# Attention in units of two heads, scores computed two units ahead, and the routing's Exp moved ahead of its token copies

## The reference

```python
probs = jax.nn.softmax(jnp.einsum('bnd,de->ben', h, router).astype(jnp.float32), axis=1)
gates, idx = lax.top_k(probs, cap)      # 16 experts, cap = 64 of 512 tokens
xs = h[bidx, idx]
```

## Time and profile before

| what | value |
|---|---|
| time, median of 3 runs | 2752.82 us (2751.13 to 2754.84) |
| the profiled execution's own time | 2752.04 us |
| its span | 2750.4 us |
| PE busy | 2445.9 us (89%) |
| DVE busy | 948.3 us (34%) |
| ACT busy | 497.1 us (18%) |
| HBM traffic | 202 GB/s over the span |

### The profile page before, as it was taken

One profiled execution on the slowest core, in us unless ns is written; L12 is line 12 of the kernel. 1 busy time (PEld: TensorE's weight loads), 2 busy tenths in 40 slices (PEclk: granted clock), 3 DMA queues, 4 the chain that ended last, 5 costly groups with the idle time before them and its releaser, 6 DMA issues.

```text
span 2750.4 us, 28001 instructions
## 1 busy us (share of the span) xinstructions
PE 2445.9 (89%) x11738; PEld 1060.6 (39%) x11738; DVE 948.3 (34%) x1631; ACT 497.1 (18%) x821; POOL 0.2 (0%) x4
## 2 busy tenths in 40 slices
PE   6899999599999988875999999889988699996698
PEld 1343345233333323332333333234433348644443
DVE  4547462411111125634011111131125745246551
ACT  2256100211110111022111111010023331124300
POOL 0000000000000000000000000000000000000000
PEclk9899999799999999977999999999998899996799
DMA  7236621599999972214899999812221120120062
GB/s 269 91 137 233 244 97 65 196 410 409 409 409 409 409 285 67 69 39 192 349 409 409 409 409 409 354 52 76 77 73 59 46 70 26 48 86 20 1 199 77
DMA packets 146010, 556.58 MB, mean 202 GB/s; under 512 B 13561, under 2 KB 14073, under 8 KB 138523
## 3 DMA queue, kind: packets, MB, share of 16 engines
q1 hardware_dynamic: 139584, 538.83, 51.2%
q10 hardware_dynamic: 6300, 15.95, 1.5%
HBM read 544.26 MB, written 10.49 MB: 202 GB/s over the span
## 4 chain that ended last, share of the span: by engine, by line
PE 74%; DVE 14%; DMA 6%; ACT 4%; issue 2%; ACTq 0%; DVEq 0%; SPq 0%
PE bank L204 72%; DMA experts<-in_exp_w 5%; PE bank L207 2%; DVE residual L1354 1%; DVE softmax L2407 1%; DVE rms L1670 1%; DMA residual<-in_w_mod 1%; DVE proj L423 0%; DVE scores L2413 0%; DVE topk L1248 0%; DVE max L1247 0%; DVE squares L1320 0%; ACT wring L1282 0%; ACT squares L1314 0%; ACT L1629 0%
## 5 line engine op out<-in xcount | busy, mean ns | idle before, releaser
L204 PE MATMUL bank<-normed,wring 128*128 128x512 f32 x1712 | 780.4, 608 | 23.7 <-DVE residual L1542 10.3
L204 PEld LDWEIGHTS bank<-normed,wring 128*128 128x128 f32 x1712 | 323.3, 193 | 425.7 <-issue 393.5
L204 PE MATMUL bank<-experts,wring 128*64 128x512 f32 x2048 | 449.6, 594 | 10.2 <-DMA experts<-in_exp_w 8.4
L204 PEld LDWEIGHTS bank<-experts,wring 128*64 128x64 f32 x2048 | 143.6, 137 | 301.2 <-issue 273.2
L1320 DVE TENSOR_TENSOR squares<-squares,bank 128x512 f32<-128x512 f32 x32 | 22.0, 688 | 688.6 <-ACT squares L1314 688.6
L204 PE MATMUL bank<-experts,hs_t 128*64 128x512 f32 x1024 | 224.1, 594 | 6.5 <-DMA experts<-in_exp_w 5.1
L204 PE MATMUL bank<-give_t,y 128*128 128x512 f32 x256 | 128.6, 621 | 10.3 <-DVE residual L1354 5.9
L204 PEld LDWEIGHTS bank<-experts,hs_t 128*64 128x64 f32 x1024 | 72.4, 137 | 147.0 <-issue 145.0
L1354 DVE SCALAR_TENSOR_TENSOR residual<-bank,mods,residual 128x512 f32<-128x512 f32 x128 | 96.1, 751 | 75.6 <-PE bank L204 69.8
L204 PE MATMUL bank<-h_tm,pick 128*128 128x512 f32 x256 | 116.8, 610 | 2.2 <-DVE pick L1262 2.2
L204 PE MATMUL bank<-proj,wring 128*128 128x512 f32 x224 | 99.4, 597 | 1.6 <-DVE proj L2470 1.6
(11 more groups left out here) (466 smaller groups left out, 2154.2 us busy)
## 6 DMA issues: line engine op xcount, KB each, us to landing
experts<-in_exp_w SPq DMA_DIRECT2D x384, 1024.0 KB, 18.4
wring<-in_w_in SPq DMA_DIRECT2D x82, 512.0 KB, 3.4
residual<-in_w_mod SPq DMA_DIRECT2D x40, 1024.0 KB, 7.0
wring<-in_cf_w SPq DMA_DIRECT2D x24, 512.0 KB, 3.4
wmod<-in_w_mod SPq DMA_DIRECT2D x8, 1024.0 KB, 10.2
merge_gates<-squares ACTq DMA_DIRECT2D x32, 256.0 KB, 3.1
merge_g<-merge_gates SPq DMA_DIRECT2D x8, 1024.0 KB, 6.5
wring<-in_w_out SPq DMA_DIRECT2D x14, 512.0 KB, 3.5
```

The lines of the kernel that those rows point to most:

```text
L204: return self.nc.tensor.matmul(out, lhsT, rhs, start=start, stop=stop, skip_group_check=True)
```

## The change

Two places are changed, and three constants with them.

Attention: 8 units (chunk c, head pair hp) replace the 16 heads. Banks 0 to 3 hold the scores of one unit, banks 4 to 7 the transposed weights and outputs. The matmuls of the two heads are issued alternately: for scores they lie on the upper and lower 64 rows of the array, for the weighted sum on the two halves of its columns. Maxima, reciprocals and gate products take both heads in one instruction. PE issues the scores of unit n+2 before the transposes of unit n; DVE issues bias and maxima of unit n+1, then the output of unit n-1, then the weights of unit n; ACT issues the Exp of unit n+1 before the copies of unit n. The three mask operations go: `cdist` now holds 1e30 where a compressed block isn't visible, and rows that see none get a gate of zero (`cseen`).

Routing: ACT runs a one-column Exp behind the shifts, then the softmax's Exp, then the eight copies. PE turns two of the eight token groups, then the probabilities, then the other six groups. DVE sets the ones while the Exp is awaited, reads the first round of the top-k straight from PSUM, and leaves out the subtraction of one, since `iota` now starts at 1.

```diff
@@ routing, tensor
+    tokens_tensor(k, m, 0)
     t.wait_ge(*k.at(f"{name}.softmax"))
     for n in range(NT):
         ins = k.turn(bank[2][0:NE, n * P:(n + 1) * P], m.pb[:, n, :])
     ins.then_inc(*k.up("tensor", f"{name}.probs"))
+    for n in range(1, NT):
+        tokens_tensor(k, m, n)
     t.wait_ge(*k.at(f"{name}.ranks"))
...
@@ routing, scalar
     modulate_scalar(k, f"{name}.h", lambda c: k.MOD[:, m.layer, 24 + c, 0:1], lambda c: k.H[:, c, :])
+    k.act(s.activation(k.SM[:, 62:63], k.con("ones", 0, 1), ACT.Exp))
+    s.wait_ge(*k.at(f"{name}.centred"))
+    k.act(s.activation(m.pb[:, :, :], m.pb[:, :, :], ACT.Exp), f"{name}.exp")
     for n in range(NT):
         for h in range(2):
             s.wait_ge(*k.at(f"{name}.h_tm{n}.{h}"))
             k.act(s.copy(m.ht[:, n, 512 * h:512 * h + 512], bank[4 + (2 * n + h) % 4][:, :]), f"{name}.ht{n}.{h}")
-    s.wait_ge(*k.at(f"{name}.centred"))
-    k.act(s.activation(m.pb[:, :, :], m.pb[:, :, :], ACT.Exp), f"{name}.exp")
@@ routing, vector
+    k.vec(v.memset(m.pet[:, :], 1.0))
     v.wait_ge(*k.at(f"{name}.exp"))
...
-    k.vec(v.tensor_copy(wk[:, 0, :], bank[2][0:NE, :]))
     for r in range(CAP // 8):
-        k.vec(v.max(m.mx[:, :], wk[:, r % 2, :]))
-        k.vec(v.match_replace(wk[:, (r + 1) % 2, :], m.mx[:, :], wk[:, r % 2, :], -1.0))
+        left = wk[:, r % 2, :] if r else bank[2][0:NE, :]
+        k.vec(v.max(m.mx[:, :], left))
+        k.vec(v.match_replace(wk[:, (r + 1) % 2, :], m.mx[:, :], left, -1.0))
...
-    k.vec(v.memset(m.pet[:, :], 1.0))
...
-    k.vec(v.tensor_scalar(wk[:, 0, :], wk[:, 0, :], -1.0, None, ALU.add), f"{name}.ranks")
```

More of the change, by code:

```diff
@@ L1580, in __init__ @@
         self.hc = n.sb("cmp_h", [P, 32])
[L1581 to L1584, removed]
+        self.sc = n.sb("scores", [P, 6, 512 + 384 + 32])
+        self.pt = n.sb("scores_t", [P, 2, 8 * P])
+        self.ms = n.sb("softmax", [P, 6, 6])
         mg = at.then()
@@ L2365, in head_scalar @@
[L2365 to L2380, removed]
-        k.act(s.copy(m.pt[:, u, i * P:(i + w) * P], bb[i // 4][:, 0:w * P]))
-    k.act(s.copy(m.pt[0:NCMP, u, j * P:(j + 1) * P], bb[j // 4][0:NCMP, (j % 4) * P:(j % 4 + 1) * P]), f"{name}.pt")
-    yield
-    yield
@@ new lines, in weights_vector @@
+def weights_vector(k, m, n):
+    v = k.nc.vector
+    c, hp, u = UNITS[n]
+    tot = m.ms[:, u:u + 2, 3:6]
+    v.wait_ge(*k.at(f"at{n}.exp"))
+    k.vec(v.reciprocal(tot, tot))
+    k.vec(v.tensor_tensor(tot, tot, m.gt[:, c, 6 * hp:6 * hp + 6].rearrange("p (h b) -> p h b", b=3), ALU.mult))
+    for e in range(2):
+        for b, (lo, hi) in enumerate(spans_of(c)):
+            x = m.sc[:, u + e, lo:hi]
+            k.vec(v.tensor_scalar(x, x, m.ms[:, u + e, 3 + b:4 + b], None, ALU.mult), f"at{n}.weights" if e and b == 2 else None)
@@ new lines, in out_heads_vector @@
+def out_heads_vector(k, m, n):
+    v = k.nc.vector
+    c, hp, u = UNITS[n]
+    cols = slice(c * P, (c + 1) * P)
+    v.wait_ge(*k.at(f"at{n}.mixed"))
+    for e, r in enumerate(HALVES):
+        k.vec(v.tensor_tensor(m.ys[r, 6 + hp, cols], k.bank[4 + 2 * e][r, 0:P], m.pj[r, NZ + hp, cols], ALU.mult),
+              f"at{n}.out" if e else None)
+def attention_vector(k, m):
[4 more added lines that the diff above has]
+            biased_vector(k, m, n + 1)
+        if n:
+            out_heads_vector(k, m, n - 1)
+        weights_vector(k, m, n)
+    out_heads_vector(k, m, last)
@@ new lines, in exponentials_scalar, with turned_weights_scalar @@
+def exponentials_scalar(k, m, n):
+    s = k.nc.scalar
+    c, hp, u = UNITS[n]
+    for b, (lo, hi) in enumerate(spans_of(c)):
+        s.wait_ge(*k.at(f"at{n}.max{b}"))
+        for e in range(2):
+            x = m.sc[:, u + e, lo:hi]
+            k.act(s.activation(x, x, ACT.Exp, bias=m.ms[:, u + e, b:b + 1], accum_out=m.ms[:, u + e, 3 + b:4 + b]),
+                  f"at{n}.exp" if e and b == 2 else None)
+def turned_weights_scalar(k, m, n):
+    s = k.nc.scalar
+    c, hp, u = UNITS[n]
+    j = len(blocks_of(m, c)[2]) - 1
+    for e in range(2):
+        bb, pt = (k.bank[4 + 2 * e], k.bank[5 + 2 * e]), m.pt[:, e, :]
+        s.wait_ge(*k.at(f"at{n}.turned{e}"))
+        for o in range(0, j, 4):
+            w = min(4, j - o)
+            k.act(s.copy(pt[:, o * P:(o + w) * P], bb[o // 4][:, 0:w * P]))
+        k.act(s.copy(pt[0:NCMP, j * P:(j + 1) * P], bb[j // 4][0:NCMP, (j % 4) * P:(j % 4 + 1) * P]), f"at{n}.pt{e}")
@@ L2509, in second_tensor @@
     fence(k, "keys", "tensor")
-    weave(None, *(heads(head_tensor, k, m, u) for u in range(NSTREAM)))
+    attention_tensor(k, m)
     fence(k, "attended", "tensor")
@@ L2545, in second_scalar @@
     fence(k, "keys", "scalar")
-    weave(None, *(heads(head_scalar, k, m, u) for u in range(NSTREAM)))
+    attention_scalar(k, m)
     fence(k, "attended", "scalar")
@@ L2596, in second_vector @@
     fence(k, "keys", "vector")
-    weave(None, *(heads(head_vector, k, m, u) for u in range(NSTREAM)))
+    attention_vector(k, m)
     fence(k, "attended", "vector")
```

127 lines of the change are left out of this document (54 added, 73 removed).

## The result

The changed kernel takes 2704.09 us (median of 4 runs, 2700.87 to 2706.66) against 2752.32 us for the kernel before (4 runs beside it, 2751.13 to 2754.84). The ratio is 0.9823, with a 95% interval of 0.9808 to 0.9838. That is 48.2 us saved; the forecast was 2701.6 us, in a range of 2691 to 2716.

The account below looks back on a forecast made before the run. PE matmuls the change doesn't touch fill about three quarters of the span; in attention no engine is the bound. 2752.0 less 16.4 (routing, two layers) and 34 (attention) gives 2701.6 us, range 2691 to 2716.

Parts of the forecast that it names:

- Routing (a), the Exp: Routing: dummy Exp hides the table load, real Exp starts about 0.1 us behind the centred logits; net 6.1 us less.
- (b): Routing: the probabilities' four transposes run at the high clock behind token transposes, some 0.6 us instead of 1.02, 0.4 less.
- (c): Routing on DVE: copy, ones and subtraction leave the chain, 1.8 us less; top-k's first PSUM reads could lose 0 to 0.5.
- (d): Routing: six late token groups and their copies lie beside the 16 us top-k and cost nothing; uncovered about 5 us.
- Attention, work: Attention on DVE: work falls from 79 us with gaps to 60.6 us, through fewer masks, maxima and small instructions.
- Pairs: Attention on PE: weighted sums of two heads run side by side on column halves, so a pair costs one.
- Attention, waits: Attention: DVE's open waits for weighted sums, 6.2 us per c = 3 unit at high clock; stage 82 us, saving 34.
- 1 (clock low throughout): Rival: the clock stays low through attention, stage 91 us, total 2710.6 us; chance 0.16.
- 3 (75 to 77): Rival: the clock rises early and attention's tail is shorter, stage 75 to 77 us, total 2693 to 2696; chance 0.12.
- 2: Rival: attention's paired matmuls don't overlap, weighted sums double, stage 93 to 98 us, total 2713 to 2718; chance 0.07.
- 4: Rival: the routing's 16 us is given back because the expert weights are the bound, total 2718 us; chance 0.03.
- 5: Rival: waits tie attention's units into one chain, stage 158 us, total 2777.6 us, slower than before; chance 0.03.

Follow-up runs that it names:

- the second profile: The changed kernel run and profiled once more with nothing changed: 2704.70 us, ratio 0.9824 to the kernel before.
- the fillers: Matmuls that nobody reads added to the changed kernel in PE's pauses, in the routings and attention's last two units: 2691.35 us, ratio 0.9775.

## Why the prediction was right, step by step

**The bound.** Right. The expert stage behind the first use of a slot kept its rate, and moving that use moved the rest of the program with it; the routing alone shows 17.1 us at the end, 1.9 of them in an attention stage that it doesn't touch.

**Routing (a), the Exp.** Right in its steps. It starts 0.10 behind `centred`, the table load is in ACT's idle time, and the ones cost 0.2 where 0.1 was taken. **(b)** The probabilities' transposes took 0.61, as forecast. **(c)** The first MAX8 from PSUM took 0.69 and its MATCH_REPLACE8 0.67 us; the later rounds, which read SBUF, take 0.68 and 0.66, so the unknown was worth nothing. **(d)** The late groups are covered: ACT's last copy of them ends at 508.6, and PE turns the slots only at 518.88.

These bring the gather's start forward by 7.7 us in the first layer (41.07 us behind the start of the norm's sum before, 33.35 after) and by 8.1 in the second, against 8.3. The 0.4 between the two layers are the logits matmuls (9.32 us, 8.93 before); counted from the centred logits the first layer has 8.1 too. They also put the first MAX8 where it stands, 0.4 later than forecast once the starts are made equal. **The missing term** is the gather's clock: the sum carried its 9.2 us over, and it took 10.0 and 9.9 (9.1 before, in the second layer). That makes 6.9 and 7.4 us, 14.3 in the two against the forecast 16.4, and below its lower end of 15.2.

**Attention, work.** Right: 55.8 us in 152 instructions for 55.5; the maxima over two heads and 1024 columns took 1.22 us. **Pairs** cost one: shown by the unpaired sums.

**Attention, waits.** Right in place, mis-sized a little. The eight gates waited 0.35, 0.35, 0, 0.57, 0.22, 0.57, 7.42 and 7.20 us, 16.7 in all. The sum had 2 x (0.5 + 1.4 + 0.2 + 6.2) = 16.6 with c = 0 and 1 at the low clock: too much at c = 1, too little at c = 3, and by chance the same in all; 2.8 us of allowance for the clock made 79.2 into 82. Measured: 55.8 + 152 x 0.03 of gaps + 16.7 = 77.1, and 3.0 left for the start, where 2.0 was taken: 80.1. **The clock** was forecast in a wrong shape: low, then high. It swung: 0.50, 0.93, 0.64, 1.00, 0.84 (0.68 over the stage; now 0.77). The last two chains lay between the 6.2 of the high level and the 9.4 of the low, the fillers brought them to 6.32, and in the kernel with attention alone they took 8.82 and 9.25. The chain's prices at both levels were right; at which level it would run was not known, and that the stage came out 2 us from the 82 is in part luck.

So attention gave 35.8 us for 34, the routing 14.3 for 16.4, 50.1 for 50.4. That these two misses nearly cancel is luck. Some 2 us (3.5 by the second profile) were lost in stretches that the sum took as unchanged, which leaves the 48.2. Of attention's 35.8, half is work: DVE has 15.4 us and 88 gaps of 0.03 less, 18 us. The other half is idle time that DVE no longer has, and it comes from the order and the pairs.

**The rivals.** 1 (clock low throughout) fell for this kernel, at 0.77, though the same attention code ran at 0.67 in the kernel with attention alone and took 83.2 us there. 3 (75 to 77) wasn't met either, at 80. 2 was tried and refuted, 4 refuted by the routing alone. 5 was false for this kernel, but its mechanism is real: taking away the bias's place ahead of the output costs 37 us, and taking away the scores' lead 50. Not tried apart from each other were the pairing of the scores, the maxima over two heads and the masks that went.

**Transposes and the clock.** The forecast went by the earlier trace rows: behind 32 transposes alone the clock stood at 1.00. The changed kernel shows it again in its last unit. PE stood idle for 3.72 us, then ran nothing but the sixteen transposes at 2554.68; the granted clock was 0.50 from 2554.6 to 2556.6, 0.68 in the next 1.4 us, and 1.00 when they had ended. The Trainium skill (TensorE: Matmul & The Clock Gate, Part 4) says that transposes do not count as PE work for the clock in the same way. The two traces don't agree with it for these 32-bit transposes, and the stage took 80 us, not the 91 of a clock that stays low.

**What stays open.** The gather took 9.82 to 10.15 us in six profiles with the same routing and the same pause of 11.86, in both layers, but 8.49 and 8.60 in the kernel with the routing alone, whose routing is the same code. In the first layer the granted clock rose 2.8 us behind the gather's start there, and 5.9 us behind it in the changed kernel. What sets that moment wasn't found. It is worth 1.2 to 1.7 us a layer, more than the dummy Exp.

## What to carry to other kernels

Where no engine is the bound and they take turns, count for each wait what the waiting engine has to do ahead of it. That work is the wait's cover. Without it the work saved here didn't show in the time at all: one moved call cost 37 us and another 50. Work out the last units by themselves, since they have no cover. When a wait ahead of matmuls is shortened or shifted, price the matmuls behind it at both clock levels. If PE has nothing to do ahead of a stretch on the critical path, as for 11.86 us here ahead of the slots and the gather and some 4 us in attention's tail, a few matmuls that nobody reads can be worth more than the next reordering (some 10 us here, against 3.5 in the stage for the output behind the weights).

## What the runs showed of the hardware beyond the expected

- The same 16 gather records took 7.1 us behind a busy PE, 9.1 to 9.4 behind pauses of 10.20 and 16.28 us, 9.8 to 10.2 behind one of 11.86, and 8.5 and 8.6 behind the same 11.86 in one kernel. A longer pause isn't always dearer.
- Filler matmuls write to a bank that nobody reads and run beside the top-k on DVE; DVE's rounds kept their 0.68 and 0.66 us.
- Sixteen transposes behind an idle PE took 3.32 us, and the weighted sums behind them ran at the high level (28 records in 1.75 us).
- The alternating matmuls on column halves run at double rate with different banks as outputs and 128-column records: 28 records in 1.75 us, where 14 of one half take 1.74.
- MAX8 and MATCH_REPLACE8 of 16x512 take the same time from PSUM (0.69, 0.67) as from SBUF.
